# Down projections: four weight differences of the sixth block product move from VectorE to GpSimd

## The reference, cut to what matters

```
def swiglu(x, w_gate, w_up, w_down):
    return (jax.nn.silu(x @ w_gate) * (x @ w_up)) @ w_down

h = x + 0.5 * rmsnorm(swiglu(rmsnorm(x, g), w_gate, w_up, w_down), g_post)     # D_MODEL 1024, D_FF 2816
```

## Time and profile before

| | |
|---|---|
| Median of 3 runs | 1069.73 us (1067.32 to 4122.85) |
| The profiled execution: its own time | 1067.87 us |
| The profiled execution: its span, first to last instruction | 1066.1 us |
| Granted TensorE clock, mean | 0.999 of full speed |
| PE busy | 1052.3 us (99%) |
| PE weight loads busy | 941.2 us (88%) |
| DVE busy | 771.8 us (72%) |
| ACT busy | 549.9 us (52%) |
| POOL busy | 45.2 us (4%) |

### The profile page before, as it was taken

How to read it: one execution, slowest core, us unless ns; L and a number is a source line. 1 busy time by engine, 2 the same in 40 slices (tenths; PEclk the granted TensorE clock), 3 DMA queues, 4 the chain that set the end, 5 groups by cost and what they waited for, 6 DMA issues and landing times.

```text
span 1066.1 us, 16095 instructions
## 1 busy us (share of the span) xinstructions
PE 1052.3 (99%) x6441; PEld 941.2 (88%) x6441; DVE 771.8 (72%) x929; ACT 549.9 (52%) x797; POOL 45.2 (4%) x98
## 2 busy tenths in 40 slices
PE   9999999999999999999999999999999999999997
PEld 7899999998888988888878888889899999988886
DVE  6988989979986573566654323458778878779964
ACT  7455455456644683577683222344444554556642
POOL 2000000000001210000000000011000000000001
PEclk9999999999999999999999999999999999999999
DMA  9523323450151554232115344315524224450051
GB/s 303 191 79 113 125 80 102 168 198 7 57 183 41 179 151 106 73 87 61 40 43 155 99 118 158 99 40 178 159 80 144 94 80 134 144 198 0 21 178 79
DMA packets 118215, 121.21 MB, mean 114 GB/s; under 512 B 6624, under 2 KB 98800, under 8 KB 118144
## 3 DMA queue, kind: packets, MB, share of 16 engines
q1 hardware_dynamic: 114928, 115.47, 34.6%
q10 hardware_dynamic: 2240, 2.11, 0.8%
q0 software_dynamic: 976, 2.66, 0.7%
HBM read 111.80 MB, written 6.29 MB: 111 GB/s over the span
## 4 chain that ended last, share of the span: by engine, by line
PE 86%; DVE 5%; ACT 3%; issue 2%; DMA 2%; SPq 1%; POOL 1%; ACTq 0%; DVEq 0%; POOLq 0%
PE bank L1777 11%; PE bank L1779 11%; PE bank L1778 11%; PE bank L1691 9%; PE bank L1681 7%; PE bank L1683 6%; PE bank L1682 6%; PE bank L1839 5%; PE bank L1840 5%; PE bank L1841 5%; PE bank L1931 1%; PE bank L1930 1%; PE bank L1929 1%; PE bank L1746 1%; PE bank L1748 1%
## 5 line engine op out<-in xcount | busy, mean ns | idle before, releaser
L1777 PE MATMUL bank<-tc,w_hi 128*128 128x256 f32 x576 | 163.0, 283 | 0.0
L1778 PE MATMUL bank<-tc,w_hi 128*128 128x256 f32 x576 | 163.0, 283 | 0.0
L1779 PE MATMUL bank<-tc,w_lo 128*128 128x256 f32 x576 | 163.0, 283 | 0.0
L1101 DVE TENSOR_TENSOR w_lo<-raw,w_hi 128x1024 fp32r<-128x1024 f32 x69 | 84.2, 1221 | 90.6 <-ACT w_hi L638 90.5
L1777 PE MATMUL bank<-u_hi,w_hi 128*128 128x256 f32 x432 | 122.5, 283 | 2.8 <-DVE scr L1295 2.8
L1779 PE MATMUL bank<-u_hi,w_lo 128*128 128x256 f32 x432 | 122.3, 283 | 0.0
L1778 PE MATMUL bank<-u_lo,w_hi 128*128 128x256 f32 x432 | 122.2, 283 | 0.0
L1681 PE MATMUL bank<-u_hi,w_hi 128*128 128x512 f32 x296 | 117.5, 397 | 0.4 <-issue 0.2
L1683 PE MATMUL bank<-u_hi,w_lo 128*128 128x512 f32 x296 | 115.6, 390 | 0.0
L1682 PE MATMUL bank<-u_lo,w_hi 128*128 128x512 f32 x296 | 115.4, 390 | 0.0
L1777 PEld LDWEIGHTS bank<-tc,w_hi 128*128 128x128 f32 x576 | 110.6, 192 | 0.0
(11 more groups left out here) (291 smaller groups left out, 2313.6 us busy)
## 6 DMA issues: line engine op xcount, KB each, us to landing
raw<-in_w_in SPq DMA_DIRECT2D x40, 512.0 KB, 3.9
raw<-in_ffn_w_down SPq DMA_DIRECT2D x20, 512.0 KB, 6.3
h<-in_ffn_w_gate SPq DMA_DIRECT2D x9, 1024.0 KB, 5.3
h<-in_ffn_w_up SPq DMA_DIRECT2D x9, 1024.0 KB, 8.9
raw<-in_ffn_w_gate SPq DMA_DIRECT2D x9, 1024.0 KB, 5.5
raw<-in_ffn_w_up SPq DMA_DIRECT2D x9, 1024.0 KB, 8.2
h<-in_ffn_w_down SPq DMA_DIRECT2D x8, 512.0 KB, 6.3
og_place<-in_ffn_w_down SPq DMA_DIRECT2D x8, 512.0 KB, 6.5
```

The source lines that it names most:

```text
L1101: V.tensor_tensor(w_lo[:, slot(u), :], raw[:, slot(u), :], w_hi[:, slot(u), :].bitcast(F32), ALU.subtract).then_inc(lo_ready, 1)
L1777: mm(dst, w_hi[:, slot(u), w], moving(n, 0, k), start=first and k == 0, stop=False, skip_group_check=True)
L1778: mm(dst, w_hi[:, slot(u), w], moving(n, 1, k), start=False, stop=False, skip_group_check=True)
L1779: last = mm(dst, w_lo[:, slot(u), w], moving(n, 0, k), start=False, stop=k == KD // 2 - 1, skip_group_check=True)
```

## The change

The branch for T4 leaves `block_weights`, and the four T4 entries leave the order of DVE. GpSimd gets a function `last_differences` with the same four subtractions, on the same tiles. All four wait until the T1 parts have been counted and, each by itself, until the `w_lo` of the fourth block product (units 12 to 15), which reads the old "21", is done. GpSimd runs it in layer 0 in front of its wait for the 16 sums, and in layer 1 behind the load of the last gain. Nothing else changes.

```diff
             def block_weights(layer, name, part):
                 d0 = U_DOWN[layer]
-                r11, r12, r21, r22 = [down_part(layer, q, part) for q in ("11", "12", "21", "22")]
+                r11, r12, r22 = [down_part(layer, q, part) for q in ("11", "12", "22")]
...
-                elif name == "T1":
+                else:
                     dve.wait_ge(w_sum, block_sums(layer) + D_SUM[2] + part)
                     dve.wait_ge(lo_ready, d0 + BLOCK_PARTS + part + 1)
                     out, x, y, op = r12, r22, r11, ALU.subtract
-                else:
-                    dve.wait_ge(w_sum, block_sums(layer) + D_SUM[2] + part)
-                    dve.wait_ge(lo_ready, d0 + 3 * BLOCK_PARTS + part + 1)
-                    out, x, y, op = r21, r21, r11, ALU.subtract
...
-                                       9: (("T2", 3),), 13: (("T1", 0),), 14: (("T1", 1),), 15: (("T1", 2),), 16: (("T1", 3),),
-                                       17: (("T4", 0),), 18: (("T4", 1),), 19: (("T4", 2),), 20: (("T4", 3),)}.get(d, ()):
+                                       9: (("T2", 3),), 13: (("T1", 0),), 14: (("T1", 1),), 15: (("T1", 2),), 16: (("T1", 3),)}.get(d, ()):
...
+            def last_differences(layer):
+
+                for part in range(BLOCK_PARTS):
+                    r21, t2 = down_part(layer, "21", part), down_part(layer, "11", part)
+                    pool.wait_ge(w_sum, block_sums(layer) + D_SUM[4] + BLOCK_PARTS - 1 + part)
+                    pool.wait_ge(lo_ready, U_DOWN[layer] + 3 * BLOCK_PARTS + part + 1)
+                    G.tensor_tensor(r21, r21, t2, ALU.subtract).then_inc(w_sum, 1)
...
             pool.wait_ge(quad_hidden, 3 * QP)
+            last_differences(0)
             pool.wait_ge(w_sum, block_sums(0) + 16)
...
             G.dma_start(g_post, gain(g2post)).then_inc(g_post_in, 16)
+            last_differences(1)
             for t in range(TT - 1):
```

## The result

| | before | changed |
|---|---|---|
| Median | 1069.59 us | 1077.64 us |
| Ratio, 95% interval | | 1.0081 (1.0058 to 1.0104) |
| The profiled execution: its own time | 1067.87 us | 1078.13 us |
| Its span | 1066.1 us | 1076.4 us |
| DVE busy | 771.8 us | 778.5 us |

The change costs 8 us, 0.8%. It stays within the 2% and inside the forecast range, but it is 3.6 us above the predicted 1074.0. Of these, 1.7 are the distance between the execution on which the forecast was built (1067.87) and the median of before (1069.59); the rise was 8.0 us where 6.1 were forecast. A second set of runs, side by side on one chip, gave 1076.32 against 1068.51, ratio 1.0081 again (1.0058 to 1.0103).

The account below looks back on a forecast made before the run. The prediction took PE (TensorE) to bound the kernel. No gain plus 3.4 and 2.5 us of PE waits, say 6.0, on the profiled 1067.87 us gave 1073.9, predicted as 1074; range 1066.8 to 1079.8.

Parts of the forecast that it names:

- The bound and the gain: Block products: PE sets the time, so the 9.1 us taken off DVE gain 0, at most 0.1 per layer.
- The price of a part: One 128x1024 subtraction of two SBUF operands on POOL: taken as 2.0 us, bounded below by 0.97.
- The row method: POOL's price from masking passes: 0.9 ns a column for each of two operands, plus 0.19 us, giving 2.0.
- VectorE waits for GpSimd: A two-operand DVE instruction waits for POOL's whole instruction, taken from a POOL 1/sqrt that took 1.61 us for 0.57.
- The objection in the earlier trace: DVE's instruction at 22.86 began 0.14 us into a POOL 1/sqrt and took its usual 1.22, which spoke for no blocking.
- The rule that whoever started first keeps the ports to its end: Trainium skill: DVE with two SBUF inputs contends with GpSimd reading SBUF; the first started keeps the shared ports until it ends.
- The order: POOL and DVE alternate from the end of w_lo 17 in layer 0, making products 18 and 19 late by 2.4 and 3.4 us.
- turns: Likeliest case, chance 0.45: POOL's parts and DVE's instructions alternate in the block products, time 1074, own range 1072 to 1078.
- Sum: 3.4 + 2.5 = 5.9: PE's waits at the block products: 3.4 us in layer 0 plus 2.5 in layer 1, say 6.0, none given back.
- No blocking: Rival, chance 0.25: DVE is not blocked, or parts are short enough; time 1067.9, at best 0.2 less.
- POOL first: Rival, chance 0.11: POOL's four parts run together while DVE waits; PE 5.4 and 4.5 us late, 1077.8.
- DVE first: Rival, chance 0.15: POOL gets only DVE's gaps, part 0 under the PSUM addition; PE waits at product 23, about 1073.

Follow-up runs that it names:

- e1_none: Changed kernel with the T4 subtraction left out, GpSimd filling only one column of each of the four tiles: 1069.03 us against 1069.59, ratio 0.9995.
- e5_alone: Changed kernel with three more 128x1024 subtractions on GpSimd in layer 0, behind the block products where VectorE has pauses: 1075.71 us, one execution.
- e7_last_part: Kernel before, with only part 3 of T4 on GpSimd and parts 0 to 2 left on VectorE: 1073.07 us against 1068.99, ratio 1.0038.
- e3_one_input: Changed kernel with T4 as 2 times quarter 21, so GpSimd reads one operand in place of two: 1068.73 us against 1068.99, ratio 0.9995.
- e6_add_sooner: Changed kernel with VectorE's first PSUM addition one unit sooner, behind unit 17 in place of 18: 1079.99 us against 1068.99, ratio 1.0098.
- e9_idle_pe: Kernel before, GpSimd idle, with VectorE making w_lo of unit 20 five times in place of once in layer 0: 1077.14 us against 1069.59, ratio 1.0074.

## Why the prediction was right, and where it fell short

- **The bound and the gain.** PE bound, VectorE's T4 parts hidden, the freed 9.1 us worth at most 0.2: e1_none has 0.1.
- **The price of a part.** Predicted 2.0 from the rows; 2.20 to 2.26 measured, in the changed kernel, in e5_alone and in e7_last_part. The Trainium skill, GPSIMD Engine Reference, Performance versus the Vector engine, gave an estimate of 2.25 by half of its 4497 ns for 2048 columns, and these runs agree with it. The row method (so many ns a column and operand) was close here by luck: for one operand it gave 1.1 us where 2.77 were measured, so its slope, from masking passes, does not carry over to arithmetic.
- **VectorE waits for GpSimd.** Taken over from the opposite direction, and right: the four lengths of 2.23 to 3.42 us. The objection in the earlier trace rows, the instruction of usual length at 22.86, was no objection: e3_one_input has a DVE instruction of usual length inside a POOL instruction too. The rule that whoever started first keeps the ports to its end came out for two operands (2.25 us), but not for one (0.84 us lost to an instruction of 2.77).
- **The order.** The forecast had turns from 277.35 on. In fact DVE kept the ports until 279.96, and turns followed. So units 17 and 18 weren't touched, and the wait fell on product 20 (3.09 us) and hardly on 19 (0.17), not on 18 and 19. This error and the low price offset each other: turns at once with 2.25 a part would be 4 x 0.25 = 1.0 more a layer, 4.4 and 3.5; e6_add_sooner, which comes near that order, has 4.2 and 3.4. The sum of waits, 5.9 us, was met, but partly by chance. SP's load behind the 16th sum started at 291.7, not at 287.7, and PE had no wait for it.
- **The missing term.** "Sum: 3.4 + 2.5 = 5.9 ... of waits of PE, and nothing gives them back" priced a wait at its length. The medians lie 8.0 and 7.8 us above before, some 2 over the waits. Of that, 0.7 lie around the waits themselves. The rest, some 1.3, fits the sequel that was left out, the stretch at 1.2 GHz: single executions lost 0, 1.6 and 2.9 us to it in layer 0, and the time of an execution goes with its clock. The clock was read in the earlier trace rows only as it stood, 1.00, and the forecast never asked what it would do behind a gap of 3 us. With the 1.7 us by which the chosen execution lay under the median of before, this makes the 3.6 us between forecast and measurement; the waits don't.
- **The rivals.** No blocking and POOL first are excluded by DVE's lengths. DVE first was right on part 0, which ran under the PSUM addition from 279.96 where that rival had 279.7, and wrong on what followed, since turns began there. So what happened is a mixture of it and of the forecast. e7_last_part shows it in pure form: the late part holds up ACT's `w_hi`, and PE waits at product 23 as that rival said.

## What to carry to other kernels

Moving a two-operand subtraction from VectorE to GpSimd beside a busy VectorE made that engine slower, not freer: each part took 1.14 us off its list and, once turns had begun, blocked its reads for 2.25. Before such a move, set the lead of the engine over the bounding one (here 0.3 to 2.5 us) against the difference, and look for a place where it works out of PSUM or has nothing to do; and if even the complete removal of the work gains only 0.1 us, as e1_none did, leave it where it is. Where the bounding engine is TensorE, price a wait of about 3 us at up to twice its length: here the 3.3 us of layer 0 cost 3.7, 5.3 and 6.6 in three executions.

## What the runs showed of the hardware that was not expected

- The ports don't pass on by fair turns. An unbroken stream of two-operand VectorE instructions kept GpSimd out for 7.3 us (9.58 - 2.25), over seven instructions. Once a VectorE instruction had been made to wait, they alternated (2.23, 2.88, 3.42 and 2.83 us for 1.22, 0.68, 1.22 and 0.68).
- A fill by GpSimd (two of 128x1024 in 1.97 us) neither waits for VectorE nor delays it. A multiplication by a constant, one operand in, takes 2.77 us but held VectorE up for only 0.84 us, once in each layer.
- The same wait of 3.09 us of TensorE was followed by a granted clock of 0.50 in one execution and of 1.00 in another of the same kernel; waits of 2.67 us went both ways too (0 and 1.4 us lost). A wait of 4.4 us caused by VectorE alone (e9_idle_pe) had the slow clock behind it as well. What decides it was not tried.
